# Two transformer blocks on one core: the split activations and what lies behind them, moved up by 32 or 64 bytes

## The chip, the cores and the metric

The kernel runs on one core of a Trainium2 chip. The metric is the device time of one execution, in microseconds (us). Every tensor named below lies in SBUF, the core's working memory of 128 partitions; a tensor has the same place, counted in bytes, in every partition.

## What is computed

The reference runs two blocks one after the other over 256 tokens of width 1024. The first is a gated linear attention with a feed-forward part; the second joins a gated delta rule and a banded attention, and has a feed-forward part with a short convolution. Cut to what matters here:

```python
def reference(x, c, ctx, c_ctx, ...):
    x = first_block(x, c, ctx, c_ctx, mod_w, ..., ffn_w_in, ffn_w_out, gla_w_in, ...)
    return second_block(x, c_2, w_ada_2, ..., w_in_2, ..., w_up_2, ..., w_down_2, ...)

def swiglu(h, w_in, w_out):              # feed-forward of the first block, hidden width 2816
    gate, up = jnp.split(h @ w_in, 2, axis=-1)
    return (jax.nn.silu(gate) * up) @ w_out
```

Nearly all arithmetic is in the products of the activations with the weight matrices. They are wanted in float32.

## The kernel before

**Products.** A weight matrix is cut into panels of 1 MB (128 partitions x 2048 float32), and the panels of all layers form one stream. SyncE loads them in halves of 1024 columns into six slots of `raw`. ScalarE rounds each half to the format float32r (`w_hi`, L969), VectorE subtracts it from the original (`w_lo`, L1481); each of the two has four slots of 4096 bytes per partition. The activations are split in the same way, into `act_hi` and `act_lo`, 16 units of 256 columns each; the hidden activations of the feed-forward parts are split into `hidden_hi` and `hidden_lo`, 22 units of 256 columns. A product is then the sum of three matmuls on TensorE, all recorded under the line of one helper (L401):

```python
def three_pass(out_, weights, moving, start, stop):
    (a_hi, a_lo), (b_hi, b_lo) = weights, moving
    for p, (a, b) in enumerate(((a_hi, b_hi), (a_hi, b_lo), (a_lo, b_hi))):
        ins = pe.matmul(out_, a, b, start=start and p == 0, stop=stop and p == 2,
                        skip_group_check=True)
```

The first operand is the stationary one, loaded by a LDWEIGHTS (PEld in the profile) while the matmul ahead of it runs; the second one streams past it and is called the moving one. `panel` (one panel of weights against the activations, 48 matmuls) has weight parts stationary and 256 columns of activations moving. `token_panel` and `token_quarter` have it the other way round: 128 columns of `act_hi` or `act_lo` stationary, 256 columns of a weight part moving. `project_hidden` has weight parts stationary and `hidden_hi` or `hidden_lo` moving. A name in the profile's rows, as `panel_banks<-act_hi,w_hi`, holds the output and then moving and stationary operand.

**Other matmuls.** The attention products, norm sums and transposes are plain float32 matmuls on tensors within `gla_work`, `ffn_work` and `mix_work`. In the second block they stand between the products of panels, which fill TensorE's time while VectorE and ScalarE prepare the next step.

**Places.** `sb(name, shape, dt, scope)` gives out places in the order of the calls, one behind the other, and takes a scope's places back at its end. So `act_hi` and `act_lo` share their place with `under_hi`, `band_q`, `under_lo`, `band_k`; and `gla_work`, the group `hidden_hi`, `hidden_lo`, `ffn_work`, and `mix_work` share one place as well, at different times. What is at which byte follows from the sizes:

```
tensor          place before   after the change
raw                    16512   16512
w_hi                   41088   41088
w_lo                   57472   57472
x_t                    73856   73856
ones                   84480   84480
rs                     90848   90848
act_hi                 93632   93664
act_lo                110016   110048
gla_work              126400   126432
mix_work              126400   126432
hidden_hi             126400   126464
hidden_lo             148928   148992
ffn_work              171456   171520
```

Within them, every operand of a product starts at a multiple of 512 bytes (a stationary one, and a token tile) or 1024 bytes (a moving one) behind the tensor's own start. Before, all these starts are multiples of 64 bytes; `rs` alone starts 32 bytes behind one.

**Order.** It is written by hand, with semaphores between the engines, and every engine works through its own list: `first`, `FILL` and the panels' numbers fix what stands where.

Of the kernel before, what the change touches and what calls it, by code (L numbers as in the profile page):

```python
# [14 lines left out]
F32 = mybir.dt.float32  # L15
# [6 lines left out]
P = 128  # L22
# [98 lines left out]
def two_blocks(nc, panels, x, ctx_x, columns, c_rows, w_glr, w_gate, w_beta_a, head_rows, rel_bias, out):  # L121
# [3 lines left out]
    with ExitStack() as ctx:  # L125
        def sb(name, shape, dt=F32, scope=ctx):
            return scope.enter_context(nc.sbuf_tensor(name, shape, dt))
# [41 lines left out]
            return cols[:, COL[name] + i:COL[name] + i + n]  # L169


        with ExitStack() as scope:
            hhi = sb("act_hi", [P, 16, T], F32R, scope)
            hlo = sb("act_lo", [P, 16, T], F32R, scope)
# [6 lines left out]
        def arena(name, size, scope):  # L181
            tensor, at = sb(name, [P, size], F32, scope), [0]

            def take(*shape, at_=None):
                n = int(np.prod(shape))
                start = at[0] if at_ is None else at_
                if at_ is None:
                    at[0] += n
                assert start + n <= size, (name, start + n, size)
                names = "abcd"[:len(shape)]  # L190
                view = tensor[:, start:start + n]
                if len(shape) > 1:
                    view = view.rearrange(f"p ({' '.join(names)}) -> p {' '.join(names)}",
                                          **{k: v for k, v in zip(names, shape)})
                return view
            take.at = at
            return take

        WORK = 25600
        with ExitStack() as scope:  # L200
# [27 lines left out]
            g_rs = take(GH, T, at_=e_at + 4096)  # L228
            assert s_at + 4096 <= WORK
        with ExitStack() as scope:  # L230
            fhi = sb("hidden_hi", [P, FT, T], F32R, scope)
            cparts = fhi[:, 0, 0:32].rearrange("p (a b) -> p a b", b=4)
            flo = sb("hidden_lo", [P, FT, T], F32R, scope)
            take = arena("ffn_work", 14000, scope)
            y1 = take(KT, T)
            sq2 = take(KT, T)
            h2 = take(KT, T)
            f_s = take(2, T)
            f_g = take(2, T)
            y3 = take(KT, T)  # L240
            f_u = take(2, 2, T)
            f_out = take(KT, T)
            c_raw = take(D)
# [1917 lines left out]
```

How the kernel before makes its waits and increments, by code:

```python
        @block.sync  # L287
        def _(sp):
            for u in range(2 * len(stream)):
                if u >= RAW:
                    kind, i = stream[(u - RAW) // 2]
                    if kind != "R":
                        sp.wait_ge(S(RELEASE[kind]), 2 * i + u % 2 + 1)
                    elif i in WHOLE_ROWS:
                        sp.wait_ge(S("rows_whole"), 2 * WHOLE_ROWS.index(i) + u % 2 + 1)
                    else:
                        sp.wait_ge(S("rows_lower"), 2 * SPLIT_ROWS.index(i) + u % 2 + 1)
                sp.dma_start(raw[:, u % RAW], panels[u // 2][:, u % 2 * HALF:u % 2 * HALF + HALF])\
                    .then_inc(S(f"landed{u % RAW}"), 16)
            for k in (0, 2, 4, 6):
                sp.wait_ge(S("out_ready"), k + 2)
                sp.dma_start(out[:, k:k + 2], f_out[:, k:k + 2]).then_inc(S("out_stored"), 16)
            sp.wait_ge(S("out_stored"), 64)
# [2 lines left out]
        @block.gpsimd  # L306
# [3 lines left out]
            def step(ins):  # L310
                made[0] += 1
                ins.then_inc(S("constants"), 1)
                pool.wait_ge(S("constants"), made[0])
# [36 lines left out]
                    pool.dma_start(wgp[32 * g + 16 * d:32 * g + 16 * d + 16, 512 * d:512 * d + 512], w_gate[d])\  # L350
                        .then_inc(S("gate_w_landed"), 16)
            pool.wait_ge(S("h1_lo"), KT)
            step(pool.memset(resets, 1.0))
# [13 lines left out]
            for n, b in enumerate((0, 2)):
                pool.wait_ge(S("decay_diff"), n + 1)
                o = dm[:, :, b * P:b * P + P]
```

## Time and profile before

| | |
|---|---|
| median of 3 runs | 1054.53 us (1053.82 to 1057.23) |
| the profiled execution's own time | 1053.46 us |
| its span, first to last instruction | 1051.4 us |
| TensorE busy | 974.7 us, 93% of the span |
| weight loads busy | 913.3 us, 87% |
| VectorE busy | 712.2 us, 68% |
| ScalarE busy | 555.8 us, 53% |
| mean granted TensorE clock | 0.966 |

Matmuls are pipelined: one of the products takes some 280 ns from start to end, but the next one starts much earlier. So the mean duration of a matmul tells little of the rate; the distance from start to start (the pitch) does, and it is found by counting how many of them a stretch of time holds. A row of a table of stretches counts every instruction that runs in the stretch, those included that began before it.

### The profile page before, as it was taken

The numbers are of one execution on the slowest core, as the hardware profiler recorded it, in microseconds if no ns is written. First come the engines' busy times: TensorE is split into PE (matmuls) and PEld (weight loads), VectorE is DVE, ScalarE is ACT, GpSimd is POOL, SyncE is SP. The second block draws the span as 40 slices with busy tenths as digits, with TensorE's granted clock in tenths as the row PEclk, the third lists the DMA queues.
The fourth block names the chain that finished last, engine by engine and source line by source line (L and its number), as shares of the span: only waits on it lengthen the run. The fifth ranks groups of instructions, "written<-read, shape, count | busy, mean of one in ns | idle before, by whom it ended". The sixth has DMA issues, their size and how long they took to land.

```text
span 1051.4 us, 19867 instructions
## 1 busy us (share of the span) xinstructions
PE 974.7 (93%) x8430; PEld 913.3 (87%) x8430; DVE 712.2 (68%) x1117; ACT 555.8 (53%) x838; POOL 25.3 (2%) x70
## 2 busy tenths in 40 slices
PE   5897999979999999799999999989998699999995
PEld 1477999869999999699798999888898599999994
DVE  2669947557777775698865543556568678888744
ACT  2658521545544533765745342656764466766433
POOL 2010000000000000210100000000000000000000
PEclk9898999998999999899999999999999889999997
DMA  9742775446888878347433436443356636556931
GB/s 328 229 130 80 244 256 186 164 137 209 284 267 287 287 264 278 138 144 248 155 121 103 145 119 170 141 157 126 120 195 213 233 103 192 182 188 191 334 96 40
DMA packets 57400, 196.78 MB, mean 187 GB/s; under 512 B 6096, under 2 KB 10592, under 8 KB 57056
## 3 DMA queue, kind: packets, MB, share of 16 engines
q1 hardware_dynamic: 51840, 187.72, 53.7%
q10 hardware_dynamic: 5216, 7.53, 2.5%
q8 instruction: 66, 1.08, 0.4%
q0 software_dynamic: 256, 0.26, 0.1%
q14 instruction: 22, 0.18, 0.1%
HBM read 194.43 MB, written 1.06 MB: 186 GB/s over the span
## 4 chain that ended last, share of the span: by engine, by line
PE 81%; DVE 9%; ACT 5%; DMA 3%; issue 1%; SPq 0%; ACTq 0%; DVEq 0%
PE panel_banks L401 68%; DMA raw<-in_panels 3%; DVE w_lo L1481 2%; PE work_banks L786 2%; ACT w_hi L969 1%; PE work_banks L614 1%; PE work_banks L573 1%; DVE raw L1514 1%; PE work_banks L715 1%; PE work_banks L757 1%; PE work_banks L546 1%; PE work_banks L869 1%; PE panel_banks L454 1%; PE work_banks L488 1%; PE work_banks L814 1%
## 5 line engine op out<-in xcount | busy, mean ns | idle before, releaser
L401 PE MATMUL panel_banks<-act_hi,w_hi 128*128 128x256 f32 (+1 forms) x1600 | 463.4, 290 | 23.6 <-DVE w_lo L1481 9.1
L401 PE MATMUL panel_banks<-act_hi,w_lo 128*128 128x256 f32 (+1 forms) x1600 | 455.0, 284 | 0.0
L401 PE MATMUL panel_banks<-act_lo,w_hi 128*128 128x256 f32 (+1 forms) x1600 | 455.0, 284 | 0.0
L1481 DVE TENSOR_TENSOR w_lo<-raw,w_hi 128x1024 fp32r<-128x1024 f32 x260 | 315.4, 1222 | 154.7 <-ACT w_hi L969 153.8
L969 ACT ACTIVATE w_hi<-raw 128x1024 fp32r<-128x1024 f32 x260 | 272.1, 1055 | 150.2 <-PE panel_banks L401 127.7
L401 PEld LDWEIGHTS panel_banks<-act_hi,w_hi 128*128 128x128 f32 x1600 | 304.8, 190 | 36.0 <-issue 20.1
L401 PEld LDWEIGHTS panel_banks<-act_lo,w_hi 128*128 128x128 f32 x1600 | 305.6, 191 | 1.9 <-issue 0.5
L401 PEld LDWEIGHTS panel_banks<-act_hi,w_lo 128*128 128x128 f32 x1600 | 304.8, 191 | 1.4
L401 PE MATMUL panel_banks<-hidden_hi,w_hi 128*128 128x256 f32 x352 | 98.6, 280 | 2.5 <-ACT hidden_hi L1186 2.5
L401 PE MATMUL panel_banks<-hidden_hi,w_lo 128*128 128x256 f32 x352 | 98.4, 279 | 0.0
L401 PE MATMUL panel_banks<-hidden_lo,w_hi 128*128 128x256 f32 x352 | 98.2, 279 | 0.0
L1514 DVE CUSTOM_DVE_ANT_0 raw<-raw,c_wide 128x1024 f32<-128x1024 f32 x80 | 94.7, 1220 | 0.3 <-DMA raw<-in_panels 0.2
L401 PEld LDWEIGHTS panel_banks<-hidden_hi,w_hi 128*128 128x128 f32 x352 | 65.9, 187 | 3.0 <-ACT hidden_hi L1186 1.7
L401 PEld LDWEIGHTS panel_banks<-hidden_hi,w_lo 128*128 128x128 f32 x352 | 66.1, 188 | 0.0
L401 PEld LDWEIGHTS panel_banks<-hidden_lo,w_hi 128*128 128x128 f32 x352 | 66.0, 188 | 0.0
L401 PE MATMUL panel_banks<-w_hi,act_hi 128*128 128x256 f32 x192 | 54.5, 284 | 2.3 <-DVE w_lo L1481 2.3
L401 PE MATMUL panel_banks<-w_lo,act_hi 128*128 128x256 f32 x192 | 53.3, 278 | 0.0
L401 PE MATMUL panel_banks<-w_hi,act_lo 128*128 128x256 f32 x192 | 53.3, 278 | 0.0
L2054 DVE SCALAR_TENSOR_TENSOR ffn_work<-panel_banks,columns,ffn_work 128x255 f32<-128x255 f32 (+1 forms) x88 | 38.4, 478 | 17.6 <-ACT ffn_work L1430 16.9
L1430 ACT ACTIVATE ffn_work<-panel_banks,columns 128x256 f32<-128x256 f32 x44 | 22.5, 561 | 31.0 <-PE panel_banks L401 31.0
L401 PEld LDWEIGHTS panel_banks<-w_hi,act_hi 128*128 128x128 f32 x192 | 36.0, 188 | 3.2 <-DVE w_lo L1481 2.5
L614 PE MATMUL work_banks<-ffn_work,ones 128*128 128x256 f32 x64 | 22.7, 493 | 17.1 <-DVE ffn_work L1707 8.1
(275 smaller groups left out, 1021.4 us busy)
## 6 DMA issues: line engine op xcount, KB each, us to landing
raw<-in_panels SPq DMA_DIRECT2D x356, 512.0 KB, 5.0
mix_work<-delta_rows ACTq DMA_DIRECT2D x2, 1024.0 KB, 10.8
x_t<-in_x ACTq DMA_DIRECT2D x1, 1024.0 KB, 9.2
gla_work<-in_ctx_x ACTq DMA_DIRECT2D x1, 1024.0 KB, 14.1
mix_work<-in_rel_bias ACTq DMA_DIRECT2D x1, 1024.0 KB, 9.9
out_x<-ffn_work SPq DMA_DIRECT2D x4, 256.0 KB, 2.5
mix_work<-in_rel_bias ACTq DMA_DIRECT2D x1, 768.0 KB, 13.9
c_wide<-in_c_rows ACTq DMA_DIRECT2D x1, 512.0 KB, 16.7
```

The source lines that it names most:

```text
L401: ins = pe.matmul(out_, a, b, start=start and p == 0, stop=stop and p == 2, skip_group_check=True)
L454: ins = pe.matmul(PB[0:2, a % TURNS, 0:256], cact[:, 0:2, 4 * h + k], raw[:, u % RAW, k * 256:k * 256 + 256], start=(h == 0 and k == 0), s ...
L488: ins = pe.matmul(MB[:, 0, :], ones[:, 0:P], sq1[:, k, :], start=(k == 0), stop=(k == 3))
L546: ins = pe.matmul(MB[:, h, t * T:t * T + T], g_k3[:, 4 * d + h, t * P:t * P + P], g_q3[:, 4 * d + h, :], start=(d == 0), stop=(d == 1))
L573: ins = pe.matmul(MB[:, (h + 2) % 4, v * T:v * T + T], g_v[:, n, h * GDV + v * P:h * GDV + v * P + P], g_a[:, h, n, :], start=(n == 2 and ...
L614: ins = pe.matmul(MB[:, bank, 0:T], ones[:, 0:P], src[:, k, :], start=(k == 0), stop=(k == 6 + tiles - 1))
L786: ins = pe.matmul(o, lhs[half, m, :], rhs[half, m, :], start=True, stop=True)
L969: act.activation(whi[:, v_ % PARTS, :], raw[:, u % RAW, :], ACT.Copy)\
L1430: ins = act.activation(f_u[:, i % 2, m, :], b[:, m * T:m * T + T], ACT.Identity, scale=col("conv_ffn_2", 88 + 22 * m + i), bias=col("b_con ...
L1481: dve.tensor_tensor(wlo[:, v_ % PARTS, :], raw[:, u % RAW, :], whi[:, v_ % PARTS, :].bitcast(F32), ALU.subtract)\
L1514: dve.tensor_tensor_reduce(raw[:, u % RAW, :], raw[:, u % RAW, :], cwide[:], 1.0, 0.0, ALU.mult, ALU.add, dst).then_inc(S("accumulated"), 1)
L2054: ins = dve.scalar_tensor_tensor(o, b[:, m * T:m * T + T - s], col("conv_ffn_2", 44 * (2 - s) + 22 * m + i), o, ALU.mult, ALU.add)
```

## The change

Two tensors of 8 float32 (32 bytes in a partition) are allocated that nothing uses: one ahead of `act_hi`, which stays allocated, so that everything behind it moves up by 32 bytes; and one in the scope of the feed-forward tensors ahead of `hidden_hi`, so that this group moves up by 64 bytes in all.

```diff
+        sb("act_home", [P, 8])
         with ExitStack() as scope:
             hhi = sb("act_hi", [P, 16, T], F32R, scope)
             hlo = sb("act_lo", [P, 16, T], F32R, scope)
...
         with ExitStack() as scope:
+            sb("hidden_home", [P, 8], F32, scope)
             fhi = sb("hidden_hi", [P, FT, T], F32R, scope)
             cparts = fhi[:, 0, 0:32].rearrange("p (a b) -> p a b", b=4)
             flo = sb("hidden_lo", [P, FT, T], F32R, scope)
```

No instruction is added, removed or moved: each engine's list has the same instructions in the same order, with other addresses in them. `raw`, `w_hi`, `w_lo`, `x_t`, `ones` and `rs` stay where they are.

## Rows read from the trace of the kernel before

**Rows 1.** The page, busy time of the engines and slices of the span.

```profile
PE 974.7 (93%) x8430; PEld 913.3 (87%) x8430; DVE 712.2 (68%) x1117; ACT 555.8 (53%) x838; POOL 25.3 (2%) x70
...
PEclk9898999998999999899999999999999889999997
```

**Rows 2.** The chain that ended last, shares of the span.

```profile
PE 81%; DVE 9%; ACT 5%; DMA 3%; issue 1%; SPq 0%; ACTq 0%; DVEq 0%
PE panel_banks L401 68%; DMA raw<-in_panels 3%; DVE w_lo L1481 2%; PE work_banks L786 2%; ACT w_hi L969 1%; PE work_banks L614 1%; PE work_banks L573 1%; DVE raw L1514 1%; PE work_banks L715 1%; PE work_banks L757 1%; PE work_banks L546 1%;
```

**Rows 3.** Groups of TensorE's instructions by shape: xcount, busy, mean ns, idle before.

```profile
L401 PE MATMUL panel_banks<-act_hi,w_hi 128*128 128x256 f32 x1568 | 450.5, 287 | 23.6 <-DVE w_lo L1481 9.1 <-DVE act_lo L1677 6.5 <-DVE act_lo L1679 6.1
...
L401 PE MATMUL panel_banks<-hidden_hi,w_hi 128*128 128x256 f32 x352 | 98.6, 280 | 2.5 <-ACT hidden_hi L1186 2.5
...
L401 PE MATMUL panel_banks<-w_hi,act_hi 128*128 128x256 f32 x192 | 54.5, 284 | 2.3 <-DVE w_lo L1481 2.3
...
L401 PE MATMUL panel_banks<-act_hi,w_hi 128*128 128x512 f32 x32 | 12.9, 403 | 0.0
```

**Rows 4.** Stretches, L401 alone: PE busy (xcount), clock, DMA share, GB/s.

```profile
131.20:141.20 10.00, 10.00 (x90) 1.00 0.90 352
145.20:155.20 10.00, 10.00 (x87) 1.00 0.85 271
158.60:168.60 10.00, 10.00 (x91) 1.00 0.47 144
176.10:186.10 10.00, 10.00 (x87) 1.00 0.58 171
300.00:310.00 10.00, 10.00 (x87) 1.00 0.83 286
380.00:390.00 10.00, 10.00 (x88) 1.00 0.84 283
...
900.00:910.00 10.00, 10.00 (x87) 1.00 0.55 172
```

**Rows 5.** Further stretches, L401 alone: PE and PEld busy (xcount).

```profile
518.55:525.00 6.45, 6.45 (x58) 6.45 (x58) 1.00 0.27 83
...
664.40:677.40 13.00, 13.00 (x117) 13.00 (x116) 1.00 0.81 269
679.10:689.30 10.20, 10.20 (x93) 10.20 (x92) 1.00 0.31 105
```

**Rows 6.** Timeline of TensorE at 130.6 us, start and duration in us.

```profile
130.76 0.28 PE L401 MATMUL panel_banks<-w_hi,act_lo 128*128 128x256 f32 x1
130.87 0.28 PE L401 MATMUL panel_banks<-w_hi,act_hi 128*128 128x256 f32 x1
131.00 0.28 PE L401 MATMUL panel_banks<-w_lo,act_hi 128*128 128x256 f32 x1
131.12 0.28 PE L401 MATMUL panel_banks<-w_hi,act_lo 128*128 128x256 f32 x1
131.23 0.28 PE L401 MATMUL panel_banks<-w_hi,act_hi 128*128 128x256 f32 x1
```

**Rows 7.** Stretches with all work: PE, PEld, DVE, ACT, POOL busy (xcount), clock, DMA.

```profile
243.60:366.20 122.60, 122.60 (x1043) 122.60 (x1043) 90.83 (x127) 60.67 (x88) 0.00 (x0) 1.00 0.82 274
...
847.90:970.40 122.50, 122.50 (x1042) 122.50 (x1041) 103.36 (x178) 82.64 (x138) 0.00 (x0) 1.00 0.57 180
```

**Rows 8.** VectorE and ScalarE on operands at either start: mean ns or min/median/max.

```profile
L1727 DVE TENSOR_TENSOR ffn_work<-ffn_work,rs x8: 682/684/693, 226.6 to 438.1; 128x512 f32<-128x512 f32 x8
...
L1983 DVE TENSOR_TENSOR mix_work<-mix_work 128x512 f32<-128x512 f32 x4 | 2.8, 692 | 0.1
...
L983 ACT ACTIVATE rs<-work_banks,eps x6: 473/474/687, 29.3 to 1043.7; 128x256 f32<-128x256 f32 x5, 128x512 f32<-128x512 f32 x1
...
L1155 ACT ACTIVATE ffn_work<-panel_banks,gate_cols 128x256 f32<-128x256 f32 x8 | 3.3, 472 | 0.0
```

## The prediction

> **What bounds the kernel now.** I read the shares of busy time first: TensorE is busy in 93% of the span, VectorE in 68%, ScalarE in 53% [rows 1]. The chain that ended last agrees: 81% of it is TensorE, and the products of L401 alone are 68%, that is 0.68 x 1051.4 = 715 us [rows 2]. So the number that decides is how far apart these products start. Their groups [rows 3] give the counts: with the activations moving, 1568 triples of 256 columns (4704 matmuls) and 32 triples of 512 (96); with the hidden activations moving, 352 triples (1056); with the weights moving and the activations stationary, 192 triples (576). Together 6432.
>
> Their durations, some 280 ns, are pipelined and say nothing of the rate, so I count them in stretches of 10 us in which L401 is busy without a break and the clock is granted in full (1.00, the 2.4 GHz level) [rows 4]. A stretch also counts the matmuls that were running at its start, 0.28 us / 0.115 us = 2.4 of them. The reader is to see that there are two rates and none between: 90 or 91 matmuls in 10 us from 131.2 and 158.6 us, 87 or 88 from 145.2, 176.1, 300, 380 and 900 us. The long stretches give the pitches closely: 13.00 us / (117 - 2.4) = 113.4 ns [rows 5] and 122.60 us / (1043 - 2.4) = 117.8 ns [rows 7]. The difference is 4.4 ns, 3.7%.
>
> The two rates are not two kinds of work. The four stretches from 131 to 186 us are the four token panels, the same code on tensors with the same starts modulo 512 bytes, and they alternate between fast and slow. They do not follow the load of the memory either: the fast stretch at 131.2 us has DMA at 352 GB/s, the slow one at 900 us has 172 GB/s. In [rows 6] one can see how it begins: starts at 130.76 and 130.87, one that comes late (131.00, 0.13 behind), and from 131.12 on the steady 0.11. A small delay moved the stream of moving columns against the stream of weight loads (a load starts with every matmul, and PEld is as unbroken as PE in [rows 5]), and from then on the faster rate held until the next break. I read this as two streams of reads which at one mutual position get in each other's way and at another do not. That is an inference; the trace shows the two rates and the late start, not the collision.
>
> **The change part by part.** Nothing is executed more or less. What can change is the cost of reads and writes whose operand starts have moved.
>
> (a) Products with the activations moving. The stationary operand stays at a multiple of 64 bytes, the moving one now starts 32 bytes behind such a multiple: the two streams are shifted against each other by 8 columns, a mutual position that no L401 row of before has. The pitch there is unknown. Below, it is bounded by 113.4 ns (the fast rate, the best any product shows) and above by the worst reading of the same rows, worked out under the rivals. I take the fast rate: the slow one looks like a coincidence of two aligned streams, and the shift takes that coincidence away. How many matmuls gain: 4704, less those that are fast already: 58 at 518.55, about half of the 93 from 679.10 on [rows 5], and I add a couple of dozen for shorter stretches; some 130. Of the 4574 that are left not all set the end: L401 is 715 us of the chain where 6432 matmuls of 117.8 ns would be 758 us, so 94%. The sum: 4574 x 4.4 ns x 0.94 = 18.9 us less.
>
> (b) Products with the hidden activations moving (1056, slow but for a few). They move by 64 bytes, so their starts stay multiples of 64 and are now multiples of 128, as those of `w_hi` and `w_lo` are. I count no change. If they went fast as well: 1056 x 4.4 x 0.94 = 4.4 us less. If the mutual position at 128 bytes is worse, the same bound as under (a) holds for a quarter as many.
>
> (c) Token panels (576). Here the stationary operand has moved by 32 bytes. Some two thirds are fast already (131, 158, 664 and 679 us, [rows 4, 5]). Between all fast and all slow lie 200 x 4.4 = 0.9 us of gain and 370 x 4.4 = 1.6 us of loss. I count 0. The 96 matmuls of 512 columns are worth less than 0.5 us at these rates.
>
> (d) The plain float32 matmuls on `gla_work`, `mix_work` and `ffn_work`. Lines 786, 614, 573, 715, 757 and 546 have together some 7% of the chain, 74 us [rows 2]. If they moved by the same 3.7% that would be 2.7 us either way; no row shows two rates for them, and I take 0.
>
> (e) VectorE and ScalarE on the moved tensors. `rs` lies 32 bytes behind a multiple of 64 before the change. A VectorE operation that reads it takes 684 ns, one of the same shape on aligned operands 692; a ScalarE one that writes it 474 ns, an aligned one 472 [rows 8]. So a start of this kind costs these engines nothing: 0, and a fraction of a per cent of work that is mostly hidden as bounds.
>
> (f) Can the others keep up when TensorE is faster? In the stage from 243.6 us VectorE has 90.8 us of work and ScalarE 60.7 in 122.6; in the one from 847.9 us VectorE has 103.4 and ScalarE 82.6 in 122.5 [rows 7]. A stage 3.7% shorter lasts 118 us; VectorE would be at 88%. The DMA would have to go from 274 to 285 GB/s in the first, and the kernel reaches 352 at 131.2 us [rows 4]. So the gain should not be taken back there.
>
> The sum is -18.9 us. The profiled execution took 1053.5 us with a span of 1051.4, which would become 1034.6; the median of the runs lies 1.1 above that execution, so 1035.7, rounded to 1036 us.
>
> What an access costs by its start is also a matter of pages. The Trainium skill, SBUF — State Buffer, section Specifications (TRN2), states cachelines of 16 bytes, with a penalty for each crossing to a new line. By that rule a move of 32 or 64 bytes leaves every operand crossing the same lines as often as before, and the time would stay at 1054.5; no run shown so far bears on it, and the rule does not explain why the same starts give two rates. The same notes, TensorE: Matmul & The Clock Gate, section Back-to-back issue gap, give 109.2 ns for 256 columns (N/2.4 + 2.5); by the rows the products never come closer than 113.4, so here the measurement decides.
>
> **Rivals.**
> *No change.* The two rates come from how each stretch is entered, not from addresses: the token panels alternate with equal starts. If the moved operands fall into the same two rates with the same likelihood, the time stays within 1051 to 1058 us (a few stretches may change sides: one of the long ones, 122 us, is worth 4.5 us). This is strongly supported by the alternation, and against it is only that the positions of the streams must matter for two rates to exist.
>
> *Slower, by a longer read.* At 2.4 GHz 256 columns would need 106.7 ns; the fast rate is 6.7 ns longer, which is 1/16, the time of 16 columns or 64 bytes. If the moving operand is fetched in pieces of 64 bytes with a small toll on each, an operand that starts in the middle of one touches 17 pieces and not 16. The fast rate becomes 113.4 x 17/16 = 120.5 ns, 2.7 above the slow rate of now: 4574 x 2.7 x 0.94 = 11.6, and for the 130 fast ones 130 x 7.1 = 0.9, together +12.5 us, 1067 us. If the collisions come on top, 117.8 x 17/16 = 125.2 ns: 4704 x 7.4 x 0.94 = +33 us, 1087 us. It decides as soon as the pitch of the moved products is over 118 ns. For it speaks the 1/16; against it that no other engine pays for a middle start [rows 8], and that the prefetch of one piece may be hidden.
>
> *A part of the gain.* Only some stretches find the fast rate after a break, or the float32 work loses a little: between -4 and -15 us, 1040 to 1050 us.
>
> *More gain.* The hidden products and the token panels go fast as well: -18.9 - 4.4 - 0.9 = -24.2, 1030 us.
>
> **How the numbers follow.** The activations fast, with or without the hidden ones (1028 to 1040): 0.40. A part of it: 0.12. No change: 0.20. Slower by up to 20 us: 0.18; by more: 0.10. The likeliest gives 1036, with 1028 to 1040 as its own range. The range for 8 in 10 takes in no change and the first form of the longer read: 1028 to 1067. A measurement of this kernel can tell about 0.3%, 3 us, from no change. Faster by more: 0.52; the same: 0.20; slower: 0.28.
>
> **What the profile after would show.** If (a) is right: 90 or 91 matmuls of L401 in every unbroken 10 us, at 300 us too, and the stage of 1043 rows that lasted 122.6 us ends after some 118. If (b) is right the stretch at 380 us still has 87 or 88. If the longer read is right: 85 or fewer. If nothing depends on starts: the same two counts, perhaps in other places. VectorE's and ScalarE's mean durations stay within a few ns. What would make me wrong above all is that no row of before shows this mutual position: the choice of the fast rate is an inference from two rates at one position.

## The result, and the profile after

The changed kernel takes 1063.45 us (median of 4 runs, 1062.9 to 1063.9); the kernel before took 1054.17 us in the runs beside it. The ratio is 1.0074, with a 95% interval of 1.0055 to 1.0093; it is estimated from all the runs and is not the quotient of the two medians, which is 1.0088. So the change made the kernel slower, by 9 us in the medians, where 18 us less were forecast.

The page of the kernel after, the shares of busy time and the chain (its lines are two higher than before, so L403 is the L401 of before):

```profile
span 1061.8 us, 19867 instructions
...
PE 987.1 (93%) x8430; PEld 926.1 (87%) x8430; DVE 711.8 (67%) x1117; ACT 555.8 (52%) x838; POOL 25.7 (2%) x70
...
PE 83%; DVE 10%; ACT 4%; DMA 2%; issue 1%; SPq 0%; ACTq 0%; DVEq 0%
PE panel_banks L403 70%; DVE w_lo L1483 3%; PE work_banks L788 2%; DMA raw<-in_panels 2%; ACT w_hi L971 1%; PE work_banks L616 1%; PE work_banks L575 1%; DVE raw L1516 1%; PE panel_banks L456 1%; PE work_banks L759 1%; PE work_banks L717 1%
```

TensorE is busy 12.4 us longer than in [rows 1], with the same 8430 matmuls. VectorE's and ScalarE's times are those of before within 0.4 us: the moved operands cost these two nothing that one can see.

Stretches of the kernel after, TensorE busy and its count; the first two lie in token panels, then activations, hidden activations of the first block, activations, hidden activations of the second block:

```profile
134.00:144.00 10.00, 10.00 (x87) 1.00 0.85 327
150.00:160.00 10.00, 10.00 (x87) 1.00 0.85 292
300.00:310.00 10.00, 10.00 (x85) 1.00 0.88 301
380.00:390.00 10.00, 10.00 (x86) 1.00 0.78 273
900.00:910.00 10.00, 10.00 (x86) 1.00 0.55 176
1000.00:1010.00 10.00, 10.00 (x87) 1.00 0.91 346
```

Against [rows 4] the reader is to see that no stretch holds 90 or 91 any more, and that those at 300 and 900 us hold 85 or 86 where they held 87. The count is coarse, so for the rest of this document I take the distance from each start of an L401 matmul of 256 columns to the next start, averaged over those below 130 ns (what is longer holds a wait, another matmul or the clock at its 1.2 GHz level). "Shift" is how far the tensor lies from its place in the kernel before.

| kernel | shift of act / hidden | activations moving | hidden, first block | hidden, second block | token panels |
|---|---|---|---|---|---|
| before | 0 / 0 | 117.7 | 117.8 | 117.6 | 114.9 |
| after | 32 / 64 | 119.9 | 120.0 | 118.7 | 118.6 |

With about 4500, 525, 525 and 563 such distances the sum of the losses is 4500 x 2.2 + 525 x 2.2 + 525 x 1.1 + 563 x 3.7 = 13.7 us. The span grew by 10.4 from one profiled execution to the other.

### The profile page after: what moved, and what is told of

It reads as the page before. It is cut to its first block, busy times and chain, and to the rows that moved or that the text cites. A ratio compares the mean times of both kernels' runs of the same rounds, so it can differ in the third digit from the quotient of the medians.

```text
span 1061.8 us, 19867 instructions
## 1 busy us (share of the span) xinstructions
PE 987.1 (93%) x8430; PEld 926.1 (87%) x8430; DVE 711.8 (67%) x1117; ACT 555.8 (52%) x838; POOL 25.7 (2%) x70
## 4 chain that ended last, share of the span: by engine, by line
PE 83%; DVE 10%; ACT 4%; DMA 2%; issue 1%; SPq 0%; ACTq 0%; DVEq 0%
PE panel_banks L403 70%; DVE w_lo L1483 3%; PE work_banks L788 2%; DMA raw<-in_panels 2%; ACT w_hi L971 1%; PE work_banks L616 1%; PE work_banks L575 1%; DVE raw L1516 1%; PE panel_banks L456 1%; PE work_banks L759 1%; PE work_banks L717 1%; PE work_banks L548 1%; PE work_banks L871 1%; PE work_banks L490 1%; PE work_banks L816 1%
## 5 line engine op out<-in xcount | busy, mean ns | idle before, releaser
L403 PE MATMUL panel_banks<-act_hi,w_hi 128*128 128x256 f32 (+1 forms) x1600 | 467.0, 292 | 23.9 <-DVE w_lo L1483 9.0
L403 PE MATMUL panel_banks<-act_lo,w_hi 128*128 128x256 f32 (+1 forms) x1600 | 459.3, 287 | 0.0
L403 PE MATMUL panel_banks<-act_hi,w_lo 128*128 128x256 f32 (+1 forms) x1600 | 458.7, 287 | 0.0
L403 PEld LDWEIGHTS panel_banks<-act_hi,w_hi 128*128 128x128 f32 x1600 | 305.7, 191 | 36.8 <-issue 20.2
L403 PEld LDWEIGHTS panel_banks<-act_lo,w_hi 128*128 128x128 f32 x1600 | 305.7, 191 | 2.1 <-issue 0.5
L403 PEld LDWEIGHTS panel_banks<-act_hi,w_lo 128*128 128x128 f32 x1600 | 305.7, 191 | 1.6
L403 PE MATMUL panel_banks<-hidden_hi,w_hi 128*128 128x256 f32 x352 | 99.3, 282 | 2.2 <-ACT hidden_hi L1188 2.2
L403 PE MATMUL panel_banks<-hidden_hi,w_lo 128*128 128x256 f32 x352 | 99.7, 283 | 0.0
L403 PE MATMUL panel_banks<-hidden_lo,w_hi 128*128 128x256 f32 x352 | 99.5, 283 | 0.0
L403 PEld LDWEIGHTS panel_banks<-hidden_hi,w_hi 128*128 128x128 f32 x352 | 66.5, 189 | 2.8 <-ACT hidden_hi L1188 1.7
L403 PEld LDWEIGHTS panel_banks<-hidden_hi,w_lo 128*128 128x128 f32 x352 | 66.4, 189 | 0.0
L403 PEld LDWEIGHTS panel_banks<-hidden_lo,w_hi 128*128 128x128 f32 x352 | 66.2, 188 | 0.0
L403 PE MATMUL panel_banks<-w_hi,act_hi 128*128 128x256 f32 x192 | 55.1, 287 | 2.2 <-DVE w_lo L1483 2.2
L403 PE MATMUL panel_banks<-w_lo,act_hi 128*128 128x256 f32 x192 | 53.9, 281 | 0.0
L403 PE MATMUL panel_banks<-w_hi,act_lo 128*128 128x256 f32 x192 | 53.9, 281 | 0.0
L403 PEld LDWEIGHTS panel_banks<-w_hi,act_hi 128*128 128x128 f32 x192 | 36.3, 189 | 3.1 <-DVE w_lo L1483 2.5
```

## The experiments

All kernels of a group ran on one chip beside the kernel before.

**First group.** Three theories were on the table. P (pieces): a moving operand that starts off a multiple of 64 bytes is fetched in one more piece. R (relative): the distance between the two streams that TensorE reads counts. E (entry): only what TensorE did just before a stream counts. A measuring kernel runs matmuls alone; its core is

```python
for m, s in PLACES:                 # shifts of the moving and the stationary operand
    for e in ENTRIES:               # 0, 64, 128, 256 columns of a float32 matmul ahead
        if e:
            pe.matmul(MB[:, 0:e], flat[:, 0:P], flat[:, 0:e], start=True, stop=True)
        stream(m, s, 16).then_inc(S("ended"), 1)        # 16 times the three passes
        made += 1
        pe.wait_ge(S("again"), made)
```

> This kernel computes none of the blocks; it returns x as it came. TensorE alone runs 100 short streams of 48 float32r matmuls of the three-pass kind (128 columns stationary, 256 moving), with w_hi, w_lo, act_hi and act_lo at the places they have in the kernel before, and with the moving operand shifted by 0, 8, 16, 32, 48, 64, 96, 128, 192, 256, 384, 512 and 768 bytes, then the stationary one by 16 to 512, then both by the same 32 to 256. Each is entered four ways: behind a wait, and behind a float32 matmul of 64, 128 or 256 columns. Theory P (pieces: a moving operand that starts off a multiple of 64 bytes touches one more piece): 113.4 or 117.8 ns at 0, 64, 128, 192, 256, 384, 512, 768; 120.0 at 8, 16, 32, 48, 96; no effect of the stationary shift. Theory R (relative: the cost follows the distance between the two streams): equal pitches for equal distances, so the pairs shifted together give 113.4 or 117.8 like 0 and 0, and a stationary shift costs as much as a moving one. Theory E (entry: starts do not matter, only how a stream begins): the four entries differ, the shifts do not.

One stream each of this kernel behind a wait, TensorE busy (count). In this order: moving shift 48, moving 32, then both operands shifted by 32, 64 and 256, then moving 64, stationary 64, stationary 192:

```profile
134.70:140.46 5.76, 5.74 (x48) 1.00 0.00 0
108.56:114.59 6.03, 6.02 (x48) 1.00 0.00 0
571.24:577.18 5.94, 5.92 (x48) 1.00 0.00 0
597.01:602.95 5.94, 5.92 (x48) 1.00 0.01 3
648.51:654.44 5.93, 5.92 (x48) 1.00 0.00 0
159.75:165.72 5.97, 5.96 (x48) 1.00 0.00 0
416.70:422.74 6.04, 6.02 (x48) 1.00 0.00 0
493.85:499.82 5.97, 5.96 (x48) 1.00 0.01 3
```

The count is the same in each, so the busy time compares them: 0.28 us over 47 distances is 6 ns. Averaged over the last 36 distances of each stream, the unshifted pair runs at 117.8 ns behind all four entries, a moving shift of 32 at 120.0, one of 48 at 113.3, both behind all four. Shifting both operands by 32, 64, 128 or 256 bytes gives back 117.8. A stationary shift alone changes the pitch (64: 120.0). P asked for 120.0 at 48 and for no effect of the stationary place, so this is against P twice over; equal rates behind all entries and different ones at different places are against E in its pure form. A moving shift of 64 runs at 118.6 (three entries) and 120.0 (one), a stationary 192 at 118.6 to 118.8.

```diff
# hidden_64_alone
+            sb("hidden_home", [P, 16], F32, scope)
             fhi = sb("hidden_hi", [P, FT, T], F32R, scope)
# all_64
+        sb("act_home", [P, 16])
         with ExitStack() as scope:
             hhi = sb("act_hi", [P, 16, T], F32R, scope)
# weights_too_32
+        sb("w_home", [P, 8])
         whi = sb("w_hi", [P, PARTS, HALF], F32R)
```

> Only the feed-forward group (hidden_hi, hidden_lo, ffn_work) moved, by 64 bytes; act_hi, act_lo and gla_work, mix_work where they were. Theory P: all starts are multiples of 64, so nothing changes: 1054 us, 117.8 ns in the hidden products. Theory R: the hidden products take the pitch they have in the changed kernel (120.0 in the first block, 118.7 in the second), the rest stays: 1056 (1055 to 1057). Theory E: 1054.

> act_hi and all behind it moved by 64 bytes, nothing by 32. Theory P: multiples of 64 everywhere, so the kernel before: 1054 us, 117.8 ns with activations moving. Theory R: another distance between the streams, so another pitch, as the hidden products have it in the changed kernel: 118.7 to 120.0 ns, 1058 to 1064 us. Theory E: 1054.

> w_hi and everything behind it moved by 32 bytes, so that the distance between weight parts and activations is that of the kernel before, and all of them start 32 bytes behind a multiple of 64. Theory P: every moving operand touches one more piece, token panels too: 120.0 ns everywhere in L401, 1066 us (1064 to 1068). Theory R: 117.8 and 113.4 ns as before, 1054 us. Theory E: 1054.

| kernel | shift of act / hidden | activations | hidden 1 | hidden 2 | token | ratio (interval) |
|---|---|---|---|---|---|---|
| hidden_64_alone | 0 / 64 | 117.7 | 118.7 | 118.6 | 115.1 | 1.0015 (0.9997 to 1.0032) |
| all_64 | 64 / 64 | 118.8 | 118.7 | 118.7 | 118.7 | 1.0054 (1.0031 to 1.0076) |
| weights_too_32 | 32 / 32, weights 32 too | 117.6 | 117.8 | 117.8 | 115.1 | 1.0013 (0.9994 to 1.0032) |

P falls again: all starts at multiples of 64 and yet 118.8 (all_64), all starts 32 bytes off and yet 117.6 (weights_too_32). E falls with all_64. R stands in all three, with one miss: in hidden_64_alone the first hidden stage ran at 118.7 ns, where 120.0 had been expected; more on these two rates below. In weights_too_32 the activations still lie 32 bytes up, but every distance to the weights is that of before (the hidden parts are 32 up as well, not 64), and with that the loss of the change is gone.

**Second group.**

> As the first measuring kernel (TensorE alone, the output is x as it came), with finer steps: the moving operand shifted by 0 to 124 bytes in steps of 4, then the stationary one by 4 to 124. Theory R with a period of 128 bytes: a stationary shift of s gives the pitch of a moving shift of 128 - s; 113.3 ns around a moving shift of 48 and, if that is the middle of a window, at 44 and 52 too; 120 at 32. Theory P: the same pitch at all moving shifts but 0 and 64, none from the stationary ones. Theory W (words: each start has a pitch of its own, no distance behind it): no agreement between s and 128 - s.

One stream each behind a wait: moving shifts of 44, 48, 52, then stationary shifts of 80, 32, 96 and 64.

```profile
317.26:323.30 6.04, 6.02 (x48) 1.00 0.01 3
343.42:349.18 5.76, 5.74 (x48) 1.00 0.00 0
368.50:374.62 6.12, 6.11 (x48) 1.00 0.01 3
...
1356.52:1362.49 5.97, 5.95 (x48) 1.00 0.01 3
1045.97:1051.85 5.88, 5.86 (x48) 1.00 0.00 0
1460.45:1466.42 5.97, 5.95 (x48) 1.00 0.01 3
1253.61:1259.63 6.02, 6.01 (x48) 1.00 0.00 0
```

48 is a single point, not the middle of a window: 120.0 at 44, 113.3 at 48, 121.9 at 52. And R with a period of 128 bytes fails: a stationary 80 gives 118.3 (busy 5.95), not the 113.3 of a moving 48.

```diff
# parts_48 (act_hi and act_lo are now views; band_q and band_k in the same way)
-            hhi = sb("act_hi", [P, 16, T], F32R, scope)
-            hlo = sb("act_lo", [P, 16, T], F32R, scope)
+            parts = sb("act_parts", [P, 8204], F32R, scope)
+            hhi = parts[:, 12:4108].rearrange("p (a b) -> p a b", b=T)
+            hlo = parts[:, 4108:8204].rearrange("p (a b) -> p a b", b=T)
...
-            fhi = sb("hidden_hi", [P, FT, T], F32R, scope)
+            hparts = sb("hidden_parts", [P, 11292], F32R, scope)
+            fhi = hparts[:, 28:5660].rearrange("p (a b) -> p a b", b=T)
# act_32_hidden_128, against the kernel before
+        sb("act_home", [P, 8])
...
+            sb("hidden_home", [P, 24], F32, scope)
```

> act_hi, act_lo, hidden_hi and hidden_lo start 48 bytes (modulo 128) behind their places in the kernel before; band_q and band_k move with them by 48, gla_work and mix_work by 64. Theory R, by the streams of the measuring kernel: 113.3 ns in all products with activations or hidden activations moving, behind any entry; about 5000 slow matmuls x 4.4 ns x 0.94 = 21 us less, 1034 us where the kernel before takes 1055 (1029 to 1040); token panels at an unknown rate, up to 2 us more. Theory P: 120.0 ns as at 32, 1066 us. Theory E (entry alone): 1054.

> The change with its second part undone: act_hi and all behind it 32 bytes up, the feed-forward group 128 bytes up instead of 64. Theory R with a period of 128 bytes: hidden products back at 117.8 ns, products with the activations moving at 120.0; (120.0 - 117.7) x 4500 x 0.94 = +9.7 us and 1 us for the token panels, so 10 to 11 us over the kernel before. If the 128-byte period is wrong, the hidden products show another pitch.

> The changed kernel itself beside the others on one chip: 9 us over the kernel before as measured at first; by theory R 10 to 11 us from the activations and 1 to 2 us from the hidden parts, so 1 to 2 us over the kernel with the hidden parts at 128 bytes.

| kernel | shift of act / hidden | activations | hidden 1 | hidden 2 | token | ratio (interval) |
|---|---|---|---|---|---|---|
| parts_48 | 48 / 176 | 113.8 | 117.2 | 117.2 | 120.0 | 0.9905 (0.9879 to 0.9932) |
| act_32_hidden_128 | 32 / 128 | 119.9 | 113.4 | 117.6 | 118.4 | 1.0065 (1.0037 to 1.0094) |
| changed_again | 32 / 64 | 119.9 | 118.7 | 118.7 | 118.6 | 1.0088 (1.0061 to 1.0116) |

The activations went as fast as the measuring kernel said. The hidden parts did not: I had placed them 48 bytes on modulo 128, which is 176 in all. So parts_48 took 1044.0 us (median of 8), where 1029 to 1040 had been expected. In act_32_hidden_128 the hidden parts were to come back to 117.8 in both blocks; the first ran at 113.4, one of the two rates that a moving shift of 128 has in lab_places (113.3 and 117.8). It was slower than the kernel before by 6.8 us in the medians, where 10 to 11 had been expected. In changed_again the first hidden stage ran at 118.7 ns, in the first profile of the same kernel at 120.0: a moving shift of 64 has these two rates in the measuring kernel as well, and a profile shows one of them. The part of the hidden products in the change's loss (changed_again against act_32_hidden_128) is 2 us in the medians, within the intervals.

**Third group.**

> As lab_fine, with shifts of 128 to 252 bytes of either operand. Lab_fine showed that a stationary shift of s does not give the pitch of a moving shift of 128 - s (113.3 at a moving 48, 118.3 at a stationary 80). Theory R256: the distance counts modulo 256 bytes. Then a moving shift of m gives here what a stationary shift of 256 - m gave there: 113.3 at moving 244 and 140, 115.6 at 184, 118.3 at 176, 116.7 at 248; and a stationary 208 gives the 113.3 of a moving 48, a stationary 192 the 118.6 or 120 of a moving 64, a stationary 204 the 121.9 of a moving 52. Theory O: each operand's own place counts, and there is no such agreement beyond chance (about one in four within 0.6 ns, since many lie at 120.0).

Streams of this kernel: a moving shift of 128 behind entries of 64, 128 and 256 columns, then moving shifts of 160, 176, 192 and 224, then a stationary 176 (each behind a wait).

```profile
36.81:42.53 5.72, 5.70 (x48) 1.00 0.00 0
43.06:48.78 5.72, 5.70 (x48) 1.00 0.01 3
49.41:55.43 6.02, 6.00 (x48) 1.00 0.00 0
...
238.65:244.60 5.95, 5.94 (x48) 1.00 0.00 0
342.74:348.65 5.91, 5.89 (x48) 1.00 0.00 0
446.79:452.82 6.03, 6.02 (x48) 1.00 0.01 3
655.43:661.32 5.89, 5.87 (x48) 1.00 0.00 0
1172.59:1178.62 6.03, 6.01 (x48) 1.00 0.01 3
```

The first three are one pair of places with two rates, 113.3 and 117.8 ns. The kind of entry does not settle which: behind a wait the same pair ran at 117.8 in lab_places and at 113.3 here. The rows after them show places of the following table.

Pitches in ns, last 36 distances, four entries each (behind a wait, then behind 64, 128 and 256 columns), from lab_fine and lab_far:

| moving shift m | pitch | stationary shift 256 - m | pitch |
|---|---|---|---|
| 32 | 120.0 120.0 120.0 120.0 | 224 | 120.0 120.0 120.0 120.0 |
| 64 | 118.6 118.6 118.6 120.0 | 192 | 118.7 118.8 118.8 118.7 |
| 96 | 117.3 118.7 118.7 118.7 | 160 | 117.3 118.7 117.4 117.3 |
| 128 | 113.3 113.3 113.3 117.8 | 128 | 113.3 117.8 113.3 113.3 |
| 160 | 118.2 118.3 118.3 118.3 | 96 | 118.4 118.3 118.5 118.3 |
| 192 | 120.0 120.0 120.0 120.0 | 64 | 120.0 120.0 120.0 120.0 |
| 224 | 116.7 116.7 116.7 116.7 | 32 | 116.7 116.7 116.7 117.8 |
| 48 | 113.3 113.3 113.3 113.3 | 208 | 120.0 118.3 120.0 120.0 |
| 140 | 117.8 117.8 118.3 117.8 | 116 | 113.3 113.5 113.5 113.3 |
| 176 | 117.1 117.1 117.1 117.1 | 80 | 118.3 118.3 118.3 118.4 |

At all seven multiples of 32 a moving shift of m has a rate within 0.2 ns of one that a stationary shift of 256 - m has (a second rate sometimes shows on one side alone: 120.0 at a moving 64, 117.8 at a stationary 32). In lab_places moving shifts of 256, 512 and 768 give 117.8 like 0, and 384 gives 113.3 and 117.8 like 128. So at multiples of 32 the distance counts, modulo 256. Between them it does not: of the 56 other pairs 18 come within 0.6 ns at some entry, and pairs put together at random would do so 17 times. So R256, as expected there for all shifts, is half right. Below 32 bytes each operand's own start counts as well.

```diff
# full_48, against parts_48: the hidden parts at 48 modulo 256
-            hparts = sb("hidden_parts", [P, 11292], F32R, scope)
-            fhi = hparts[:, 28:5660].rearrange("p (a b) -> p a b", b=T)
+            hparts = sb("hidden_parts", [P, 11324], F32R, scope)
+            fhi = hparts[:, 60:5692].rearrange("p (a b) -> p a b", b=T)
# act_140, against full_48: 35 for 12 in the places of act_parts
-            hhi = parts[:, 12:4108].rearrange("p (a b) -> p a b", b=T)
+            hhi = parts[:, 35:4131].rearrange("p (a b) -> p a b", b=T)
```

> As parts_48, with the hidden parts 48 bytes modulo 256 behind their old place (in parts_48 it was 176, and they ran at 117.2 ns). Theory R256: 113.3 ns in both hidden stages, 3.8 ns x 1050 x 0.95 = 3.8 us less than parts_48, which was 0.9905 of the kernel before: 0.987. Theory O or a period of 128: 117.2 as in parts_48.

> Activation parts 140 bytes behind their old place, hidden parts 48. In the token panels the activations are stationary, so there the distance is that of a moving shift of 128 - 140 = 244 modulo 256. Theory R256, from the stationary shifts of 12 and 116 in lab_fine: 113.3 to 113.5 ns in both kinds, token panels 6.5 ns faster than in parts_48: 563 x 6.5 x 0.95 = 3.5 us less than full_48, 0.984 of the kernel before, unless an entry finds the 120.0 that one of four found at 12. Theory O: no such pair.

| kernel | shift of act / hidden | activations | hidden 1 | hidden 2 | token | ratio (interval) |
|---|---|---|---|---|---|---|
| full_48 | 48 / 48 | 113.8 | 113.4 | 113.4 | 120.0 | 0.9848 (0.981 to 0.9886) |
| act_140 | 140 / 48 | 118.3 | 113.5 | 113.6 | 120.4 | 1.0024 (0.9999 to 1.0049) |

In act_140 the hidden parts keep their place of full_48, by 36 for 60 in `hidden_parts`, which begins 96 bytes higher there. full_48 is the fastest of all: 1038.9 us (median of 4) where the kernel before took 1055.2. act_140 missed (1.0024 where 0.984 was expected): I had inferred the rate of a moving 140 from a stationary 116, and lab_far, on record in the same group, shows 117.8 for the moving one. Its token panels settled at 113.3, 120.0, 123.3 and 123.3 ns; a stationary 12 shows the first two of these in lab_fine, and not the third.

Stretches of full_48: activations, hidden, activations, hidden, then token panels.

```profile
300.00:310.00 10.00, 10.00 (x91) 1.00 0.84 265
380.00:390.00 10.00, 10.00 (x90) 1.00 0.86 302
900.00:910.00 10.00, 10.00 (x91) 1.00 0.60 198
1000.00:1010.00 10.00, 10.00 (x91) 1.00 0.01 2
155.00:165.00 10.00, 10.00 (x87) 1.00 0.45 163
```

The table of places foretells nearly every other stage too, once one counts the distances. A token panel has the roles exchanged: activations stationary at 192 modulo 256, weights moving at 128, which is the distance of a moving shift of 128 in the measuring kernel. That is the one with the rates 113.3 and 117.8, and the token panels of [rows 4] take one or the other of them in turn. After the change this distance is that of a shift of 96, with 117.3 and 118.7: the four token panels settled at 118.7, 118.7, 117.3 and 120.0, in changed_again just so again; the 120.0 is a rate that my four entries had not found. In full_48 it is a stationary 176: 120.0 in both. The hidden parts of parts_48, a moving 176: 117.2 in both blocks where the measuring kernel has 117.1. One more rate lies outside the table: in the kernel before, 60 products with the activations moving ran at 113.4 ns from 518.6 us on (the 58 of [rows 5]), at the unshifted place, for which all four entries of the measuring kernels give 117.8. The kernel after has no stretch of products with the activations moving below 119 ns.

## Why the prediction was wrong

**What held.** TensorE's product stream is the bound; among the distances of TensorE's matmuls that were compared the change moves those of L401 only; nothing is executed more or less; VectorE and ScalarE pay nothing for the new starts (`hidden_lo` from `hidden_hi`, all of them moved by 64 bytes: 418 ns after and before; `hidden_hi` 410 and 408); and plain float32 matmuls on `gla_work` and `mix_work`, which have moved too, start as far apart as before: at the full clock 216 ns on average for 256 columns (L573 of before), 113 for 128 (L757) and 30 for 64 (L786), in the kernel before, after and in full_48 alike. So the nothing of (d) holds for these. The two rates are two rates of one pair of places, and a stretch that has settled on one keeps it.

**The step that failed is (a): "the slow one looks like a coincidence of two aligned streams, and the shift takes that coincidence away".** At the distance that 32 bytes give, the pitch is 120.0 ns behind every entry, above both rates of before: where the sum has 4574 x 4.4 ns less, the trace has some 4500 x 2.2 ns more. The rows of before showed only two of the distances (the activations' 0, and the token panels', which is that of a shift of 128), so they could not say what a third would do. The unshifted products at 113.4 ns that the prediction counted (the 58 and half of the 93 of [rows 5]) showed only that the unshifted place has the better rate too, now and then. I took the better end as the nearest row, with no reason in a row; the two rates were evidence that position matters, not of the direction.

**The rival with the longer read had the size and not the mechanism.** The prediction gave slower by up to 20 us a chance of 0.18. The rival gave 120.5 ns and +12.5 us; measured were 120.0 ns and +9.3 us. But a further piece is not the cause: with everything 32 bytes off, the weights too, the pitch is 117.6 (weights_too_32), and a start 48 bytes off is the fastest of all. Its number agreed by chance.

**Step (b), no change in the hidden products,** was wrong too: a shift of 64 is another distance, modulo 256, with 118.7 or 120.0 ns for 117.8; 525 x 1.1 + 525 x 2.2 = 1.7 us in the first profile, before what stands beside them. **Step (c)** was mis-sized: the token panels lost 3.7 ns each, 563 x 3.7 = 2.1 us, where at most 1.6 us had been bounded by the two rates of before.

**The factor of 0.94 was too high for this change.** It stood for the share of the longer or shorter distances that reaches the end. 13.7 us of longer distances became 9.3 us in the medians, about two thirds (the interval of the ratio allows 6 to 10 us). In full_48 the changes are 4500 x 3.8 + 525 x 4.4 + 525 x 4.2 - 563 x 5.1 = 18.7 us, and the median beside the kernel before is 16.3 us less, nearly nine tenths (12 to 20 us). The spans of the kernel before alone lie between 1045 and 1057 us, so the second share is hardly known.

Following the n-th matmul in the traces of before and after shows where some of the rest goes. In unbroken stages 300 matmuls lose 0.67 us, which is 300 x 2.2 ns. Here are the same pieces of the chain of waits, before, after and in full_48:

```profile
237.74 127.44 PE panel_banks L401 x1056
366.90 61.05 PE panel_banks L401 x516
...
842.06 121.72 PE panel_banks L401 x1008
```

```profile
243.65 127.73 PE panel_banks L403 x1050
373.09 62.20 PE panel_banks L403 x516
...
850.75 123.02 PE panel_banks L403 x1008
```

```profile
239.47 122.83 PE panel_banks L402 x1056
364.01 58.81 PE panel_banks L402 x516
...
835.43 116.41 PE panel_banks L402 x1008
```

The second piece runs at the full clock in all three and changes by the pitch alone: 1.15 us more is 516 x 2.2 ns, 2.24 us less is 516 x 4.4. The first (which holds six matmuls fewer in the kernel after) and the third grow by less than their pitch because they also begin at the 1.2 GHz level, and the kernel after stays there for a shorter time (3.1 us of the first piece where the kernel before has 5.8, and 3.4 of the third where it has 5.6).

The largest step back lies between the 3600th matmul (507 us) and the 3900th (551 us): 1.8 us. There stand the norm sums behind the last q, k, v panel. These are the groups of TensorE's instructions with the idle time before them, in before, after and full_48, and a stretch of before and one of after with the granted clock behind the count:

```profile
L715 PE MATMUL work_banks<-mix_work,ones 128*128 128x512 f32 x16 | 8.9, 710 | 2.1 <-ACT mix_work L1266 2.1
L717 PE MATMUL work_banks<-mix_work,ones 128*128 128x512 f32 x16 | 7.3, 598 | 1.4 <-ACT mix_work L1268 1.4
L716 PE MATMUL work_banks<-mix_work,ones 128*128 128x512 f32 x16 | 9.0, 716 | 3.7 <-ACT mix_work L1267 3.7
...
513.20:516.60 3.40, 3.35 (x4) 0.50 0.46 148
...
521.00:526.00 5.00, 5.00 (x22) 1.00 0.60 187
```

Two things differ. The slower product stream comes later to a point at which ScalarE sets the time, and waits 0.7 us less there; the faster one comes earlier and waits 1.6 us more. And in the kernel before the clock, behind 2.1 us in which TensorE was idle, fell to the 1.2 GHz level for 3.4 us, so that the sums took 1.6 us longer than in the kernel after, where it did not fall. The second is not a matter of the pitch alone: in weights_too_32 the pitches and the wait (2.1 us) are those of before, the clock did not fall there, and the sums took 7.3 us. Over all runs beside each other the changed kernel was granted more of the clock than the kernel before (medians 0.971 of 8 runs and 0.965 of 21), full_48 as much as it (0.9665 of 4 and 0.967 of 13). How much of the missing third is clock and how much is waiting no run separates.

From the 3900th matmul to the 5100th (613 us), in the delta rule's solve, only 0.2 us are lost; but only 166 of the distances counted here lie in it, worth 0.4 us. That L401 stands in the chain with 68% says where time passes, not that all of it shrinks with the pitch.

**Two pages against the runs.** The Trainium skill, SBUF — State Buffer, section Specifications (TRN2), states cachelines of 16 bytes and a penalty for each crossing to a new one. By it nothing would change here; the runs show 120.0, 113.3 and 117.8 ns at 32, 48 and 0, which are all multiples of 16, so here it does not decide. The Trainium skill, TensorE: Matmul & The Clock Gate, section Step-by-step: what each phase is for, holds that the two read ports of TensorE are independent, and that loading the next weights takes no read bandwidth from the running matmul. A stationary shift of 64 bytes alone takes the pitch from 117.8 to 120.0 ns in lab_places, so the place of what is loaded does change the matmuls' rate; the runs do not show how.

**What stays open.** Why the distance counts modulo 256 bytes, why 48 is fast and 44 and 52 are not, and what at an entry picks one of two rates: the kind of entry alone does not. That the two read streams collide in SBUF is an inference from the table of places; no run shows the collision. A place that is fast for both roles of the activations was not found.

## What to carry to other kernels

When a kernel is one long stream of matmuls, count the starts in stretches of equal length before anything else: if equal work shows two rates, operand places are worth a sweep, and allocating eight unused floats is an edit with a cost that can go either way. Sweep the places of the stationary and the moving tensor in a small kernel of its own (a quarter of a millisecond covers ten places), with several entries each, and place the tensors by its table. Use only pairs that it has measured: the table foretold nearly every stage here, while reasoning from two known rates got the sign wrong, and so did inferring a moving shift of 140 from a stationary one. And do not expect the whole sum of the pitches in the span: where another engine sets the time a faster stream only waits longer, and the granted clock can differ between the two kernels.

## What the runs showed of the hardware

- The distance between starts of float32r matmuls of 256 columns, back to back at the 2.4 GHz level, settles between 113.3 and 123.3 ns, a span of 9%, by the places of the two operands and by how the stream begins (measuring kernels; token panels of act_140). 113.3 ns was the lowest anywhere.
- When the operands are shifted by multiples of 32 bytes, the distance between them modulo 256 decides which rates there are (7 of 7 pairs, and 117.8 ns for both shifted alike by 32, 64, 128 or 256); with finer steps it does not (18 of 56 pairs, where chance gives 17).
- Some pairs of places have two steady rates (a moving shift of 128: 113.3 or 117.8; of 64: 118.6 or 120.0; the unshifted pair: 117.8, and 113.4 for 60 matmuls of the kernel before), and a stream keeps the one it settled on for as long as it is not broken, 1042 matmuls in a row at 117.8 from 243.6 us in the kernel before. What the four entries of the measuring kernel show is not the whole list: the fourth token panel of the changed kernel settled at 120.0 where they had 117.3 and 118.7.
- The same shifts did not show in VectorE's and ScalarE's operations (`hidden_lo` 418 ns before and after, `hidden_hi` 408 and 410), nor in the distance between plain float32 matmuls of `gla_work` and `mix_work` (216, 113 and 30 ns for 256, 128 and 64 columns).
- The granted clock differed between two kernels that differ in places alone: medians 0.965 before and 0.971 in changed_again. At one point of the profiled executions 3.4 us at the 1.2 GHz level, behind 2.1 us of an idle TensorE, made the norm sums 1.6 us longer; weights_too_32 has the same wait and no such stretch.
